# Shift and scale of the first norm computed by blocks of 128 features, with the first q and k products begun among the blocks

## What is computed

```python
ada = jax.nn.silu(c) @ w_ada[l] + b_ada[l]            # c: (1, 1024), w_ada: (1024, 6144)
sh1, sc1, g1, sh2, sc2, g2 = jnp.split(ada, 6, axis=-1)
h = modulate(rms_norm(x, norm1_pre[l]), sh1, sc1)     # normed * (1 + sc1) + sh1
y = token_mixer(h, w_in[l], ...)
...
proj = h @ w_in                                       # q, k, v and eight more parts
qk = jax.nn.silu(causal_dwconv(jnp.concatenate([q, k], axis=-1), conv_qk_w))
```

## Time and profile before

| | us |
|---|---|
| median of 3 runs | 1257.64 |
| lowest, highest | 1256.55, 1258.28 |
| the profiled execution | 1258.15 |
| its span | 1256.3 |
| TensorE busy | 1132.1 (90%) |
| VectorE busy | 911.9 (73%) |
| ScalarE busy | 510.4 (41%) |

### The profile page before, as it was taken

How to read it: one execution, slowest core, us unless ns; L and a number is a source line. 1 busy time by engine, 2 the same in 40 slices (tenths; PEclk the granted TensorE clock), 3 DMA queues, 4 the chain that set the end, 5 groups by cost and what they waited for, 6 DMA issues and landing times.

```text
span 1256.3 us, 14902 instructions
## 1 busy us (share of the span) xinstructions
PE 1132.1 (90%) x5180; PEld 792.6 (63%) x5180; DVE 911.9 (73%) x1807; ACT 510.4 (41%) x994; POOL 336.4 (27%) x320
## 2 busy tenths in 40 slices
PE   5999999999899898987887887886798999999998
PEld 4989999998664454443333433332345887888887
DVE  5997987786888766776667766677766786788544
ACT  3657453545433122221222222221524477677442
POOL 4000000001455544544544455444441000000000
PEclk9999999999999999998999999899999999999999
DMA  8874577588999999999999999999998522455550
GB/s 356 335 281 189 174 289 281 213 319 322 367 424 427 427 426 428 426 428 426 427 427 427 427 427 426 427 427 427 428 426 338 202 101 100 169 201 174 195 201 34
DMA packets 58703, 406.70 MB, mean 324 GB/s; under 512 B 7012, under 2 KB 7220, under 8 KB 10500
## 3 DMA queue, kind: packets, MB, share of 16 engines
q0 software_dynamic: 39184, 273.55, 51.8%
q1 hardware_dynamic: 19444, 132.19, 28.1%
HBM read 404.66 MB, written 1.06 MB: 323 GB/s over the span
## 4 chain that ended last, share of the span: by engine, by line
PE 53%; DMA 29%; DVE 9%; issue 4%; ACT 3%; POOL 2%; SPq 0%; DVEq 0%; POOLq 0%
PE bank L861 12%; DMA row_place<-in_peer_uv,ei 10%; DMA wq_place<-in_peer_uv,ei 8%; DMA gbuf<-in_peer_uv,ei 6%; PE bank L503 5%; PE bank L507 5%; PE bank L504 5%; PE bank L1020 5%; DMA ring<-in_peer_uv,ei 2%; PE bank L1023 2%; PE bank L1050 2%; PE bank L1051 2%; PE bank L1052 2%; PE bank L780 2%; PE bank L528 2%
## 5 line engine op out<-in xcount | busy, mean ns | idle before, releaser
L861 PE MATMUL bank<-gbuf,dg 128*128 128x512 f32 x504 | 246.3, 629 | 64.1 <-ACT dg L1349 56.7
L1545 DVE TENSOR_TENSOR half<-ring,half 128x1024 fp32r<-128x1024 f32 x175 | 212.7, 1222 | 85.4 <-ACT half L1076 83.5
L1076 ACT ACTIVATE half<-ring 128x1024 fp32r<-128x1024 f32 x173 | 181.8, 1056 | 127.8 <-PE bank L1052 47.0
L861 PEld LDWEIGHTS bank<-gbuf,dg 128*128 128x128 f32 x504 | 97.5, 199 | 197.3 <-issue 116.4
L2064 DVE CUSTOM_DVE_ANT_0 gbuf<-gbuf,h2t 128x1024 f32<-128x1024 f32 x126 | 154.4, 1226 | 78.0 <-DMA gbuf<-in_peer_uv,ei 75.2
L2432 POOL DMA_INDIRECT gbuf<-in_peer_uv,ei x123 | 145.2, 1180 | 175.9 <-PE bank L861 107.5
L1341 ACT ACTIVATE za<-za 128x4 f32<-128x4 f32 x60 | 12.3, 205 | 387.5 <-DVE za L2064 380.0
L503 PE MATMUL bank<-hh,half 128*128 128x256 f32 x448 | 113.0, 290 | 0.6 <-DVE hl L1703 0.3
L504 PE MATMUL bank<-hl,half 128*128 128x256 f32 x448 | 110.5, 284 | 0.0
L861 PE MATMUL bank<-ring,dg 128*128 128x512 f32 x192 | 94.4, 620 | 11.7 <-ACT dg L1349 10.1
L861 PE MATMUL bank<-wq_place,dg 128*128 128x512 f32 x200 | 95.2, 613 | 10.4 <-ACT dg L1349 9.5
(11 more groups left out here) (455 smaller groups left out, 2079.4 us busy)
## 6 DMA issues: line engine op xcount, KB each, us to landing
ring<-in_weights SPq DMA_DIRECT2D x116, 1024.0 KB, 5.1
gbuf<-in_weights SPq DMA_DIRECT2D x4, 1024.0 KB, 10.2
gbuf<-in_peer_uv,ei POOLq DMA_INDIRECT x129, 20.8
bcs<-in_b_ada POOLq DMA_DIRECT2D x3, 512.0 KB, 9.0
xs<-in_x SPq DMA_DIRECT2D x2, 512.0 KB, 3.9
ya<-in_weights SPq DMA_DIRECT2D x1, 1024.0 KB, 18.0
qkT<-in_weights SPq DMA_DIRECT2D x1, 1024.0 KB, 19.9
pad<-in_weights SPq DMA_DIRECT2D x2, 512.0 KB, 20.0
```

The source lines that it names most:

```text
L861: r = e.matmul(acc[a][j][:, :], dg[:, i % 4, :], expert_rows(i)[:, 1024 + 512 * j:1536 + 512 * j], start=h == 0 and k == 0, stop=h == 7 an ...
L1076: e.activation(h, v, AF.Copy).then_inc(*o.inc(*highs_of(n)))
L1545: e.tensor_tensor(l, v, h.bitcast(f32), ALU.subtract).then_inc(*o.inc(s_lov, split(n)))
```

## The change

The eight loads `("adc", j)` now hold, for all 1024 rows, 128 columns of the shift and the 128 of the scale of the same features. Between them stand the two loads of q, so that the list begins adc 0, 1, 2, q 0, adc 3, 4, q 1, adc 5, 6, 7. For block j VectorE multiplies and adds row groups 0 to 3 (128x256 each, `ada_part`), and TensorE does row groups 4 to 7 itself: weights straight from the load's tile, multiplied by one column of `cs` (`ada_columns`, 8 matmuls), then two more for VectorE's part (`ada_columns_rest`). VectorE forms the block's shift and scale, ScalarE scales it and writes its high half, VectorE the low half. Between the blocks TensorE does those steps of the products of chunks 0 to 2 (`early`) whose feature blocks are there: 63 of their 72 matmuls, the last 9 after block 7. Chunks 3 to 7 follow as before. Slots and banks of the first ten loads and eight products come from new tables (`EARLY`, `QK_BANK`). `keep_busy(8)` runs once, ahead of the first block; the other nine are gone.

```diff
     for j in range(8):
-        plan(("adc", j), "w_ada", 256 * (j % 4), 1024 * (j // 4), 2)
-    plan_f("q", "w_in", 3072, 512)
+        plan(("adc", j), "w_ada", 0, 128 * j, 8)
+        if j in (2, 4):
+            plan(("q", j // 2 - 1), "w_in", 0, 3072 + 256 * (j // 2 - 1), 8, "cols")
...
+    EARLY = (3, 4, 0, 1, 2, 5, 3, 6, 7, 4)
+    QK_BANK = (4, 7, 0, 3, 1, 2, 0, 3)
...
# TensorE
-        for c in range(2):
-            e.wait_ge(s_k0, c + 1)
-            for pb, fs in ((banks[5], range(8)),) if c == 0 else ((banks[6], range(4)), (banks[7], range(4, 8))):
-                column_sums(pb, acc2[c], fs, True, False)
-            if c == 0:
-                e.wait_ge(s_acc, 4)
-                column_sums(banks[5], accd[:, 0, :], range(8), False, True).then_inc(*o.inc(s_ada0, 1))
-        e.wait_ge(s_acc, 7)
-        keep_busy(3)
-        for i in range(2):
-            e.wait_ge(s_acc, 8 + i)
-            column_sums(banks[6 + i], accd[:, 1, :], range(4 * i, 4 * i + 4), False, True).then_inc(*o.inc(s_ada0, 2 + i))
-            keep_busy((1, 5)[i])
...
+        def ada_columns(j):
+
+            pb, w = banks[5 + j % 2], slot(ADC[j])
+            if j >= 2:
+                e.wait_ge(s_S1, 2 * j - 2)
+            e.wait_ge(*arrived(ADC[j]))
+            for c in range(4, 8):
+                for side in range(2):
+                    e.matmul(pb[:, side:side + 1], w[:, c, 128 * side:128 * side + 128], cs[:, c:c + 1],
+                             start=c == 4 and side == 0, stop=False, skip_group_check=True)
+
+        def ada_columns_rest(j):
+
+            pb = banks[5 + j % 2]
+            e.wait_ge(s_acc, j + 1)
+            for side in range(2):
+                r = e.matmul(pb[:, side:side + 1], accd[:, j % 2, 128 * side:128 * side + 128], ones_f[:, 0:1], start=False,
+                             stop=True, skip_group_check=True)
+            r.then_inc(*o.inc(s_ada0, j + 1))
...
+            for k in range(k0, k1):
+                e.wait_ge(s_fhi, FHI["h", k])
+                e.matmul(pb[:, 0:256], hi[:, k, :], hh[:, k, :], start=k == 0, stop=False)
+                e.wait_ge(s_flv, FLV["h", k])
+                e.matmul(pb[:, 0:256], hi[:, k, :], hl[:, k, :], start=False, stop=False)
+            e.wait_ge(s_lov, split(c))
+            for k in range(k0, k1):
+                e.matmul(pb[:, 0:256], lo[:, k, :], hh[:, k, :], start=False, stop=False)
+
+        e.wait_ge(s_cs, 1)
+        keep_busy(8)
+        steps = {2: ((0, 0, 2),), 3: ((0, 2, 3), (1, 0, 3)), 4: ((0, 3, 4), (1, 3, 4)), 5: ((0, 4, 5), (1, 4, 5), (2, 0, 5)),
+                 6: ((0, 5, 6), (1, 5, 6), (2, 5, 6)), 7: ((0, 6, 7), (1, 6, 7), (2, 6, 7))}
+        for j in range(8):
+            ada_columns(j)
+            if j == 0:
+                x_columns()
+            ada_columns_rest(j)
+            for step in steps.get(j, ()):
+                early(*step)
...
# ScalarE
+        for j in range(8):
+            scaled(j)
+            if j in (1, 2, 4):
+                hi((1, 2, 4).index(j))
...
         for g in range(8):
-            taken("qk"[g // 4], g % 4)
-            e.activation(pad[:, g, 3:259], banks[g % 4][:, 0:256], AF.Copy).then_inc(*o.inc(s_pad, g + 1))
+            n = chunk_at["qk"[g // 4], g % 4]
+            if g == 0:
+                hi(n + 3)
+            for m in ahead(n) if g > 1 else []:
+                hi(m)
+            e.wait_ge(s_chunk, n + 1)
+            e.activation(pad[:, g, 3:259], banks[QK_BANK[g]][:, 0:256], AF.Copy).then_inc(*o.inc(s_pad, g + 1))
...
# VectorE
+        def ada_part(j):
+
+            acc, w = accd[:, j % 2, 0:256], slot(ADC[j])
+            if j >= 2:
+                e.wait_ge(s_ada0, j - 1)
+            e.wait_ge(*arrived(ADC[j])) if j < 7 else e.wait_ge(s_adc, 16)
+            e.tensor_scalar(acc, w[:, 0, :], cs[:, 0:1], None, ALU.mult).then_inc(*o.inc())
+            for c in range(1, 4):
                 e.wait_ge(*o.now)
+                e.scalar_tensor_tensor(out=acc, in0=w[:, c, :], scalar=cs[:, c:c + 1], in1=acc, op0=ALU.mult,
+                                       op1=ALU.add).then_inc(*o.inc(s_acc if c == 3 else None))
...
+        for j in range(8):
+            ada_part(j)
+            if j:
+                scaled_lo(j - 1)
+            scale(j)
+            if j in (2, 3, 4):
+                lo(j - 2)
+        scaled_lo(7)
...
# GpSimd
-        e.wait_ge(s_acc, 9)
+        e.wait_ge(s_ada0, 7)
         e.memset(pad[:, :, 0:3], 0.0).then_inc(*o.inc(s_const, 2))
-        e.wait_ge(s_S1, 2)
+        e.wait_ge(s_S1, 16)
...
# SyncE
             if name[0] == "adc":
-                e.wait_ge(s_acc, i + 1 if i < 7 else 9)
-                if i % 4 == 0:
-                    e.wait_ge(s_k0, i // 4 + 1)
+                e.wait_ge(s_ada0, name[1] + 1)
```

More of the change, by code:

```diff
@@ new lines, in tensor_program @@
+        e.wait_ge(s_fhi, FHI["h", 7])
+        for c in range(3):
+            hi, lo = chunk_of(c)[2:]
+            e.matmul(qk_pb[c][:, 0:256], hi[:, 7, :], hh[:, 7, :], start=False, stop=False)
+            e.matmul(qk_pb[c][:, 0:256], lo[:, 7, :], hh[:, 7, :], start=False, stop=False)
+        e.wait_ge(s_flv, FLV["h", 7])
+        for c in range(3):
+            hi = chunk_of(c)[2]
+            e.matmul(qk_pb[c][:, 0:256], hi[:, 7, :], hl[:, 7, :], start=False, stop=True).then_inc(*o.inc(s_chunk, c + 1))
+            frees[QK_BANK[c]] = ((s_pad, c + 1),)
@@ L612, in tensor_program @@
+        for g in range(3, 8):
+            product("qk"[g // 4], g % 4, QK_BANK[g], hh, hl)
+            frees[QK_BANK[g]] = ((s_pad, g + 1),)
         gp = bank(6)
@@ L1676, in vector_program @@
-        for i in range(2):
-            e.wait_ge(*((s_adc, 16), arrived(7))[i])
-            if i:
-                e.wait_ge(s_acc, 8)
-            for k in (6, 7):
-                ada_more(7, k, H2[i], s_acc if k == 7 else None)
-        e.wait_ge(s_ada0, 1)
-        e.tensor_tensor(ada[:, 0:8], banks[5][:, 0:8], bada[:, 0:8], ALU.add).then_inc(*o.inc())
-        def scale(i):
-            s_ = slice(8 + 4 * i, 12 + 4 * i)
-            e.wait_ge(s_ada0, 2 + i)
-            e.tensor_tensor(ada[:, s_], banks[6 + i][:, 4 * i:4 * i + 4], bada[:, s_], ALU.add).then_inc(*o.inc())
-            e.wait_ge(*o.now)
-            e.scalar_tensor_tensor(out=S1[:, 4 * i:4 * i + 4], in0=ada[:, s_], scalar=1.0, in1=n1pre[:, 4 * i:4 * i + 4],
-                                   op0=ALU.add, op1=ALU.mult).then_inc(*o.inc(s_S1, 1 + i))
@@ new lines, in scale, with scaled_lo @@
+        def scale(j):
+            pb = banks[5 + j % 2]
+            e.wait_ge(s_ada0, j + 1)
+            e.tensor_tensor(ada[:, j:j + 1], pb[:, 0:1], bada[:, j:j + 1], ALU.add).then_inc(*o.inc(s_S1, 2 * j + 1))
+            e.scalar_tensor_tensor(out=S1[:, j:j + 1], in0=pb[:, 1:2], scalar=ada[:, 8 + j:9 + j], in1=n1pre[:, j:j + 1],
+                                   op0=ALU.add, op1=ALU.mult).then_inc(*o.inc(s_S1, 2 * j + 2))
+        def scaled_lo(j):
+            e.wait_ge(s_fhi, FHI["h", j])
+            e.tensor_tensor(hl[:, j, :], cg[:, j, :], hh[:, j, :].bitcast(f32), ALU.subtract).then_inc(
+                *o.inc(s_flv, FLV["h", j]))
@@ L1721, in vector_program @@
             n = chunk_at["qk"[g // 4], g % 4]
-            for m in ahead(n):
+            if g == 0:
+                lo(n + 3)
+            for m in ahead(n) if g > 1 else []:
                 lo(m)
```

162 lines of the change are left out of this document (56 added, 106 removed).

## The result

The changed kernel takes 1275.12 us in the median of four runs (1272.18 to 1275.77), the kernel before 1257.10 beside it (1255.15 to 1258.28, four runs). The ratio is 1.0133, 95% interval 1.0119 to 1.0148: slower, by 18.0 us between the medians. The profiled execution took 1275.77, with a span of 1273.9.

A forecast was written before the change was run, and what follows sets the result against it. TensorE was taken to bind the changed start: 11.4 load + 34.4 columns + 3.45 transposes + 15.3 products + 1.2 waits = 65.8 us, against 41.2; loss 24.6, less 3 for clock, 21.6, giving 1279 us (1276 to 1283).

The forecast's parts named there:

- What bounds before: Transfers, then VectorE, bind the start up to 37 us; any shift of VectorE's first convolution moves all that follows.
- The column pass at 0.215: TensorE's single-column matmuls: 0.215 us a pass, 160 passes 34.4 us against 13.8 before, 4.3 us a block.
- Rival 3: Columns hide and transfers set the end, if 160 passes fit into 16.2 us, 0.10 each: 1255; chance 0.04.
- Single-column work does not raise the clock: TensorE's column passes in the start stay at the low clock though the engine is busy; 24.6 us lost at low clock throughout.
- rival 2: The page's rule holds, TensorE at the high level throughout the start: loss 4.2 us, 1262; chance 0.06.
- Rival 1: Columns don't raise TensorE's clock but hold it once a wide burst has: loss 9 to 17 us, 1266 to 1275; chance 0.14.
- One rise, worth 3 us: One TensorE clock rise behind the 21 wide matmuls at about 47 to 51.5 us, giving back about 3 us.
- The waits: TensorE in the start: handovers of about 0.05 each and one wait for a low half, some 1.2 us.
- What before has in its place: Behind the three chunks come chunk 3's high and low halves; after equals before where the chunks end at 41.2 us.
- VectorE, ScalarE and SyncE hidden: In the blocks, VectorE's round of some 3 us, ScalarE's part and the loads lie under TensorE's 4.3 us and products.
- Behind the start: First products again run slow for some us, mostly hidden by VectorE's 2.96 a chunk: ±1 us.
- Rival 4: No clock rise until well behind the start: 24.6 us and up to 4 more, 1283 to 1287; chance 0.13.

The follow-up runs named there:

- before_q_among: The kernel before with only the new load order, the two q loads among the w_ada loads: 1264.58 us, ratio 1.0053.
- rows_act2: Changed kernel with load order and products as before, 256-column passes, sums shared by three engines, two halves moved, keep_busy(14): 1254.80 us, ratio 0.9974 to before.
- no_cols: The changed kernel without TensorE's eight column matmuls per block (row groups 4 to 7 left out): 1266.22 us, ratio 1.0059 to the kernel before.
- loads_first: The changed kernel with q loads behind the w_ada loads and all products behind the last block, single-column blocks kept: 1267.40 us, ratio 1.0076 to before.
- rows_among: The changed kernel with TensorE's part turned round, cs as one-column weight and 256 columns streaming past: 1268.35 us, ratio 1.0076 to the kernel before.

## Why the prediction was right, step by step

The direction and the mechanism were right, and 1275.1 lies in the range; the forecast of 1279 was 3.9 too high, 0.9 outside its own band of 1276 to 1283. Part of the closeness is luck: the clock term was 4.7 too small and the waits 1.9 too small, and these two misses partly cancel.

- **What bounds before.** Right: whatever delayed the first convolution arrived at the first gather. Once the 1.14 for the low half already done is taken off in the kernels with early products, the two shifts agree within 1.0 us in ten of the eleven kernels (after 18.91 and 18.68, before_q_among 4.22 and 4.11, rows_act2 -3.16 and -3.78); in no_cols they are 6.8 and 8.6.
- **The column pass at 0.215.** Right where the clock was low: 16 passes in 3.55 us, and 20 in 4.27 in the later blocks of loads_first. It carries the forecast. Rival 3, that the passes might be quick with weights from the load's tile, is refuted by the same rows.
- **Single-column work does not raise the clock.** Right, and now shown with more than the earlier trace rows: 24.30 us of 24.30 busy at a granted clock of 0.50 (loads_first). With 256 columns a pass the clock was held at 1.00 from 8.71 to 39.43 in rows_among, and over all the blocks in rows_act2. The Trainium skill, page "TensorE: Matmul & The Clock Gate", section "Why this matters for your kernels", has continuous work bring the full clock; for single-column matmuls these traces disagree, and rival 2, which stood on that rule, did not come.
- **Rival 1, columns hold the clock once it is high.** Refuted: it fell at 39.3 and at 52.9, both times in a run of columns and with the engine busy all through (3.30 us of 3.30 just before, in both windows, with 6 and 9 wide matmuls between the columns). The time lies at the rival's upper end, for another reason, the next point.
- **One rise, worth 3 us.** This is the term that was mis-sized. There were three stretches at the high level ahead of the end, 0.84 + 3.4 + 3.4 = 7.7 us, and at twice the pace each gives back about its own length. The rise behind the large burst came as forecast (matmuls 44.35 to 48.98, high from 49.5). That behind the 12 matmuls of 32.90 to 35.60 did not enter the sum; I had compared only the longest burst with the rise of before. And `keep_busy(8)`, which I gave nothing, left the first columns 0.8 us at the high level in spite of the 2.3 idle us ahead of them.
- **The waits.** 1.2 us was for handovers and one wait for a low half (that was 0.45, at 28.18); one more of 1.93 at 43.48 was missed. VectorE's sums of block 5 stood behind chunk 2's low half, which waited 2.02 for ScalarE's high half, and that stood behind a block's scaling:

```profile
40.37 1.23 DVE L1572 TENSOR_TENSOR half<-ring,half 128x1024 fp32r<-128x1024 f32 x1 [2.02 <-ACT half L1117]
```

```profile
39.30 1.04 ACT L1117 ACTIVATE half<-ring 128x1024 fp32r<-128x1024 f32 x1
```

- **The sum again.** 65.8 at the low clock, less 0.3 (the first load was there at 11.13, not 11.40), less 7.7, plus 1.9, is 59.7; the last matmul of the three chunks ends at 59.65 + 0.57 = 60.2. Against the equal point of before, 41.2, that is 19.0, and 18.9 was measured at the first convolution.
- **What before has in its place.** Right: ScalarE's high half of chunk 3 comes right behind the chunks, and TensorE waits for it.

```profile
60.09 1.06 ACT L1117 ACTIVATE half<-ring 128x1024 fp32r<-128x1024 f32 x1 [2.07 <-PE bank L648]
```

- **VectorE, ScalarE and SyncE hidden.** Right for this kernel: VectorE waits for TensorE in each of the eight blocks, 20.8 us in all, the longest 5.1 (the waits view):

```profile
DVE ada L1703 <- PE bank L607: 20.8, 8, 5.1
```

But the cover is thin. I priced VectorE's round at some 3 us; no_cols showed 3.27 with TensorE's part gone. So relieving TensorE alone can win only part of the loss back, which I did not say.
- **Behind the start.** The first products did not run slow, since the rise at 59.8 came before them, and nothing was lost further on; 18.9 became 17.6 at the end of the span, inside the ±1 allowed but for 0.3.
- **Rival 4's time.** 24.6 over the median 1257.64 is 1282.2, so its range should read 1282 to 1286, by the same half microsecond that the forecast takes off.

The loss can be taken apart by the runs at the first convolution, each step with the former ones: early products undone 62.59 to 52.65, the load order undone to 49.46, columns made wide to 43.75, the sums shared by three engines and two halves moved to 39.38. These are steps between kernels, not prices of single causes: the second holds a wait of 2.04 and a stretch of high clock besides the load order, the third a shift and scale one block later and `keep_busy(18)`, and each mark has up to 1.0 us from the pick-up of the first load. The order of the loads by itself was only run on the kernel before, where it costs 4.2.
